# A hybrid encoder block in fp32r: rows of 256 words in the weight ring, a buffer of its own for the first group, and the scores one unit later

## The reference

```python
n1 = rmsnorm(x, norm_mix_g)
q, k, v, o_pre, if_pre, x_r, g_r = split(n1 @ w_in)   # 4 x 1024, 8 gate columns, 2 x 1024
h_m = sigmoid(o_pre) * rmsnorm_per_head(mlstm(q, k, v, i_pre, f_pre))  # 4 heads of 256
h_r = rglru(x_r) * gelu(g_r)                          # 8 blocks of 128
x = x + concat(h_m, h_r) @ w_out                      # 2048 x 2048
gate, up = split(rmsnorm(x, norm_ffn_g) @ w_up)       # 2048 x 2*5632
x = x + (silu(causal_conv3(gate)) * up) @ w_down      # 5632 x 2048
y = rmsnorm(x, norm_final_g)
```

## Time and profile before

| | us |
|---|---|
| median of 3 runs | 1154.48 (1154.33 to 1154.86) |
| the profiled execution | 1154.4 |
| its span, first to last instruction | 1152.6 |
| PE busy | 1140.6 (99%) |
| DVE busy | 746.1 (65%) |
| ACT busy | 578.2 (50%) |
| POOL busy | 51.3 (4%) |
| data moved | 213.56 MB, mean 185 GB/s |

### The profile page before, as it was taken

How to read it: one execution, slowest core, us unless ns; L and a number is a source line. 1 busy time by engine, 2 the same in 40 slices (tenths; PEclk the granted TensorE clock), 3 DMA queues, 4 the chain that set the end, 5 groups by cost and what they waited for, 6 DMA issues and landing times.

```text
span 1152.6 us, 18163 instructions
## 1 busy us (share of the span) xinstructions
PE 1140.6 (99%) x6048; PEld 972.5 (84%) x6048; DVE 746.1 (65%) x985; ACT 578.2 (50%) x769; POOL 51.3 (4%) x47
## 2 busy tenths in 40 slices
PE   8999999999999999999999999999999999999997
PEld 8888888888878888888888888888888888887885
DVE  6668585685866676666666666666666655556554
ACT  7556365463746554444344434444443544455454
POOL 0100100001000000000000000000000000001000
PEclk9999999999999999999999999999999999999999
DMA  8756648566565566566656655655665555555553
GB/s 266 230 147 205 173 142 227 146 195 184 177 204 170 175 195 188 164 195 194 190 156 211 185 180 169 212 183 165 198 195 187 187 189 189 185 187 188 188 184 109
DMA packets 166729, 213.56 MB, mean 185 GB/s; under 512 B 6940, under 2 KB 149660, under 8 KB 166576
## 3 DMA queue, kind: packets, MB, share of 16 engines
q1 hardware_dynamic: 165456, 210.40, 59.0%
q0 software_dynamic: 528, 2.17, 0.5%
q10 hardware_dynamic: 720, 0.67, 0.2%
HBM read 211.10 MB, written 2.11 MB: 185 GB/s over the span
## 4 chain that ended last, share of the span: by engine, by line
PE 91%; DVE 4%; DMA 2%; ACT 2%; issue 1%; SPq 0%; DVEq 0%; ACTq 0%
PE ps L1073 39%; PE ps L1201 27%; PE ps L1075 20%; PE ps L1070 2%; DMA raw<-w_in_dram 2%; DVE w L618 1%; PE ps L1071 1%; ACT w L352 1%; ACT xn L352 1%; PE ps L1171 0%; DVE aT L624 0%; PE ps L1145 0%; PE ps L1045 0%; PE ps L1153 0%; SPq L276 0%
## 5 line engine op out<-in xcount | busy, mean ns | idle before, releaser
L1073 PE MATMUL ps<-xT,w 128*128 128x512 f32 x2048 | 726.7, 398 | 0.0
L618 DVE TENSOR_TENSOR w<-raw,w 128x1024 fp32r<-128x1024 f32 x391 | 479.0, 1238 | 364.7 <-ACT w L352 362.9
L352 ACT ACTIVATE w<-raw 128x1024 fp32r<-128x1024 f32 (+1 forms) x393 | 409.3, 1054 | 434.6 <-PE ps L1075 265.5
L1075 PE MATMUL ps<-xT,w 128*128 128x256 f32 x2048 | 575.9, 281 | 0.0
L1073 PEld LDWEIGHTS ps<-xT,w 128*128 128x128 f32 x2048 | 385.0, 188 | 94.1
L1075 PEld LDWEIGHTS ps<-xT,w 128*128 128x128 f32 x2048 | 386.0, 189 | 0.2
L1201 PE MATMUL ps<-w,aT 128*128 128x512 f32 x1440 | 336.9, 395 | 0.3 <-DVE aT L624 0.2
L1201 PEld LDWEIGHTS ps<-w,aT 128*128 128x128 f32 x1440 | 270.2, 188 | 65.6 <-DVE aT L624 1.2
L352 ACT ACTIVATE fs<-fc 128x512 f32<-128x512 f32 x22 | 13.9, 632 | 101.2 <-DVE fc L967 101.2
L1029 POOL TENSOR_TENSOR fs<-fs,rB 128x512 f32<-128x512 f32 x22 | 28.7, 1305 | 580.4 <-ACT fs L352 580.4
L624 DVE TENSOR_TENSOR aT<-act,aT 128x256 fp32r<-128x256 f32 x88 | 39.0, 443 | 0.0
(11 more groups left out here) (146 smaller groups left out, 402.6 us busy)
## 6 DMA issues: line engine op xcount, KB each, us to landing
raw<-w_up_dram SPq DMA_DIRECT2D x176, 512.0 KB, 4.5
raw<-w_in_dram SPq DMA_DIRECT2D x95, 512.0 KB, 3.9
raw<-w_down_dram SPq DMA_DIRECT2D x88, 512.0 KB, 4.5
raw<-w_out_dram SPq DMA_DIRECT2D x32, 512.0 KB, 4.5
xres<-x_dram SPq DMA_DIRECT2D x3, 512.0 KB, 8.4
y_dram<-xn SPq DMA_DIRECT2D x3, 384.0 KB, 3.1
bc<-rows POOLq DMA_DIRECT2D x4, 256.0 KB, 6.6
gfin<-gfin_dram POOLq DMA_DIRECT2D x1, 1024.0 KB, 5.9
```

The lines of the kernel that those rows point to most:

```text
L352: return sc.activation(out_, in_, fn, **kw)
L618: v.tensor_tensor(w[:, s, :, 1, 0:COLS], raw[:, s, :].rearrange("p (c n) -> p c n", c=CH), w[:, s, :, 0, 0:COLS], ALU.subtract).then_inc(l ...
L1073: mm(full, w[:, s, c, 0, cut], xT[:, kt, :, :].rearrange("p a n -> p (a n)"), start=kt == 0, stop=False)
L1075: ins = mm(rest, w[:, s, c, 1, cut], xT[:, kt, 0, :], start=False, stop=kt == KT - 1)
```

## The change

The ring's rows become 256 words long. The first group gets a buffer of its own, w0, with rows of 272 words for all 16 k-tiles; it lies where tensors of the mixer begin (mixT, gr and others), whose order is changed so that those are in front that are first written later. With that the rounding of group 1 no longer waits for units of group 0 (empty=True).

The first group is fed by single k-tiles: TensorE, ScalarE and VectorE count steps k0 to k15 instead of t0 to t7; the first two k-tiles' weights are rounded and subtracted singly, all others in halves of a unit; and SP loads all units of group 0 in halves. The transposes of bank 1 stand ahead of the first product, the others between tiles or half units. SP issues the first half of the first weights ahead of x 256 to 511. ScalarE issues the identity first; VectorE both rounds and subtracts the gate columns and waits for their transfer; and the rest of the parameters goes to POOL's queue, behind a wait for the last piece of x. VectorE's small instructions on the parameters stand behind the whole of group 0. WARM_UP becomes 6 and KEEP_WARM 2. The scores stand behind unit s == 2 of O.

The diff, cut to its core:

```diff
-WARM_UP, KEEP_WARM = 8, 6
+WARM_UP, KEEP_WARM = 6, 2
...
-        w = sb("w", [P, RING, CH, 2, WROW], F32R)
+        w = sb("w", [P, RING, CH, 2, COLS], F32R)
...
+        first_group = ExitStack()
+        w0 = sb("w0", [P, KT, 2, WROW], F32R, where=first_group)
+        first_group.close()
...
+        def first_place(k):
+            bank = (4, 5, 6, 2)[k] if k < CH else (7, 3, 4, 5, 6, 7)[k // 2 - 2]
+            return ps[:, bank, 0:S] if k < CH else ps[:, bank, k % 2 * S:(k % 2 + 1) * S]
+        def last_in_bank(k):
+            return k if k < CH else k | 1
...
-            load_x(0)
-            sp.wait_ge(lo_ready, 1)
...
+            load_x(0, COLS, x_first_landed)
+            sp.wait_ge(lo_ready, RING)
+            load_first(0, 0, w_first_landed[0])
+            load_x(COLS, BANK, x_landed[0])
+            load_first(0, CH // 2, raw_landed[0])
             for s in range(1, RING):
-                load_x(s)
-                load(0, s, in_v[s, :, :, COL_V:COL_V + COLS], raw[:, s, :].rearrange("p (c n) -> p c n", c=CH))
+                load_x(s * BANK, (s + 1) * BANK, x_landed[s])
+                load_first(s, 0, w_first_landed[s])
+                load_first(s, CH // 2, raw_landed[s])
...
-            def round_units(group, slots=range(RING)):
+            def round_units(group, slots=range(RING), empty=False):
                 for s in slots:
                     act_e.wait_ge(raw_landed[s], group * 16 + 16)
-                    act_e.wait_ge(unit_used, group * RING + s + 1)
+                    if not empty:
+                        act_e.wait_ge(unit_used, group * RING + s + 1)
...
-            act_e.dma_start(par[:, PAR_GMIX + KT:], par_in[:, PAR_GMIX + KT:]).then_inc(par_landed, 16)
...
+            for c in range(CH // 2):
+                x_hi(c)
+                first_hi(0, c, 1, w_first_landed[0], first_hi_ready)
+            for c in range(CH // 2, CH):
+                x_hi(c)
+            first_hi(0, CH // 2, CH // 2, raw_landed[0], hi_ready)
+            for s in range(1, RING):
+                for c, landed, ready in ((0, w_first_landed[s], first_hi_ready), (CH // 2, raw_landed[s], hi_ready)):
+                    for k in range(s * CH + c, s * CH + c + CH // 2):
+                        x_hi(k)
+                    first_hi(s, c, CH // 2, landed, ready)
+                if s < RING - 1:
+                    squares(A0, s - 1, 0)
             squares(A0, 0, 1)
-            round_units(1, [0])
+            round_units(1, [0], empty=True)
...
+            dve.wait_ge(gate_landed, 16)
+            did(v.tensor_copy(w_gate[:, :, 0:2 * H], gate_flat), V0, "gw_hi")
+            after(dve, V0, "gw_hi")
+            did(v.tensor_tensor(w_gate[:, :, 2 * H:4 * H], gate_flat, w_gate[:, :, 0:2 * H], ALU.subtract), V0, "gw_lo")
             dve.wait_ge(gain_landed, 16)
+            for c in range(CH // 2):
+                x_lo(c)
+                dve.wait_ge(first_hi_ready, c + 1)
+                first_lo(0, c, 1, first_lo_ready)
...
+            pool.wait_ge(x_landed[RING - 1], 16)
+            pool.dma_start(par[:, PAR_GMIX + KT:], par_in[:, PAR_GMIX + KT:]).then_inc(par_landed, 16)
             pool.dma_start(tri, const_in[:, C_TRI:C_TRI + P]).then_inc(tri_landed, 16)
...
             transpose_x(0)
             for n in range(KEEP_WARM):
                 mm(ps[:, B_DEN, 0:P], ones[:], ones[:], start=True, stop=True)
+            transpose_x(1)
             pe.wait_ge(group_free, 1)
+            after(pe, V0, "gw_lo")
             pe.wait_ge(first_lo_ready, 1)
-            part_of_unit(0, 0, range(CH // 2), tiles=V0, gated=True)
-            transpose_x(1)
+            part_of_unit(0, 0, [0], tiles=V0)
+            pe.wait_ge(first_lo_ready, 2)
+            part_of_unit(0, 0, [1], tiles=V0)
+            transpose_x(2)
             pe.wait_ge(lo_ready, RING + 1)
...
+            part_of_unit(0, 0, [2], tiles=V0)
             transpose_x(3)
+            part_of_unit(0, 0, [3], tiles=V0).then_inc(unit_used, 1)
+            transpose_x(4)
+            for s in range(1, RING):
+                pe.wait_ge(first_lo_ready, s + 2)
+                part_of_unit(s, 0, range(CH // 2), tiles=V0)
+                if s < RING - 1:
+                    transpose_x(2 * s + 3)
+                pe.wait_ge(lo_ready, s + (1 + RING))
+                part_of_unit(s, 0, range(CH // 2, CH), tiles=V0).then_inc(unit_used, 1)
+                if s < RING - 2:
+                    transpose_x(2 * s + 4)
...
-                    if s == 1:
+                    if s == 2:
                         after(pe, V0, "gcol1")
```

More of the change, by code:

```diff
@@ L424, in _, with x_hi @@
[L424 to L435, removed]
+            def x_hi(k):
+                after(act_e, E0, f"k{last_in_bank(k)}")
+                did(act_fn(xT[:, k, 0, :], first_place(k), scale=par[:, PAR_GMIX + k:PAR_GMIX + k + 1]), A0, f"k{k}")
@@ L689, in _ @@
[L689 to L695 removed]
+            w_gate = w0[:, :, 0, COLS:WROW]
+            gate_flat = gw[:].rearrange("p k a h -> p k (a h)")
@@ new lines, in _, with x_lo @@
+            dve.wait_ge(gate_landed, 16)
+            did(v.tensor_copy(w_gate[:, :, 0:2 * H], gate_flat), V0, "gw_hi")
+            after(dve, V0, "gw_hi")
+            did(v.tensor_tensor(w_gate[:, :, 2 * H:4 * H], gate_flat, w_gate[:, :, 0:2 * H], ALU.subtract), V0, "gw_lo")
+            dve.wait_ge(gain_landed, 16)
+            def x_lo(k):
+                after(dve, A0, f"k{last_in_bank(k)}")
+                did(v.scalar_tensor_tensor(out=xT[:, k, 1, :], in0=first_place(k), scalar=par[:, PAR_GMIX + k:PAR_GMIX + k + 1],
+                                           in1=xT[:, k, 0, :], op0=ALU.mult, op1=ALU.subtract), V0, f"k{k}")
@@ new lines, in first_lo @@
+            def first_lo(s, c, n, ready):
+                tiles = slice(s * CH + c, s * CH + c + n)
+                v.tensor_tensor(w0[:, tiles, 1, 0:COLS], raw[:, s, c * COLS:(c + n) * COLS].rearrange("p (c n) -> p c n", c=n),
+                                w0[:, tiles, 0, 0:COLS], ALU.subtract).then_inc(ready, 1)
+            for c in range(CH // 2):
+                x_lo(c)
+                dve.wait_ge(first_hi_ready, c + 1)
+                first_lo(0, c, 1, first_lo_ready)
+            for c in range(CH // 2, CH):
+                x_lo(c)
@@ new lines, in _ @@
+            dve.wait_ge(hi_ready, 1)
+            first_lo(0, CH // 2, CH // 2, lo_ready)
+            for s in range(1, RING):
+                for k in range(s * CH, s * CH + CH // 2):
+                    x_lo(k)
+                dve.wait_ge(first_hi_ready, s + CH // 2)
+                first_lo(s, 0, CH // 2, first_lo_ready)
+                for k in range(s * CH + CH // 2, (s + 1) * CH):
+                    x_lo(k)
+                dve.wait_ge(hi_ready, s + 1)
+                first_lo(s, CH // 2, CH // 2, lo_ready)
@@ L1054, in spread_rows, with part_of_unit @@
                 did(ins, E, "rB")
-            def part_of_unit(s, pair, tiles_of_k, rows_out=False, tiles=None, gated=False):
+            def part_of_unit(s, pair, tiles_of_k, rows_out=False, tiles=None):
                 for c in tiles_of_k:
                     kt = s * CH + c
-                    if tiles and c % 2 == 0:
+                    if tiles is V0:
+                        after(pe, tiles, f"k{kt}")
+                    elif tiles and c % 2 == 0:
                         after(pe, tiles, f"t{kt // 2}")
@@ L1064, in part_of_unit @@
                         cut = slice(n * P, (n + 1) * P)
-                        if gated:
+                        if tiles is V0:
                             for part, high, end in ((0, 0, WROW), (1, 0, COLS), (0, 1, COLS + 2 * H)):
-                                ins = mm(ps[:, 2 * pair + n, 0:end], xT[:, kt, high, cut], w[:, s, c, part, 0:end],
+                                ins = mm(ps[:, 2 * pair + n, 0:end], xT[:, kt, high, cut], w0[:, kt, part, 0:end],
                                          start=kt == 0 and part == 0 and high == 0, stop=kt == KT - 1 and high == 1)
                         elif rows_out:
-                            mm(full, xT[:, kt, 0, cut], w[:, s, c, :, 0:COLS], start=kt == 0, stop=False)
-                            ins = mm(rest, xT[:, kt, 1, cut], w[:, s, c, 0, 0:COLS], start=False, stop=kt == KT - 1)
+                            mm(full, xT[:, kt, 0, cut], w[:, s, c, :, :].rearrange("p a n -> p (a n)"), start=kt == 0, stop=False)
+                            ins = mm(rest, xT[:, kt, 1, cut], w[:, s, c, 0, :], start=False, stop=kt == KT - 1)
                         else:
@@ L1076, in part_of_unit, with unit @@
                 return ins
-            def unit(g, s, pair, rows_out=False, tiles=None, gated=False):
+            def unit(g, s, pair, rows_out=False, tiles=None):
                 pe.wait_ge(lo_ready, g * RING + (s + 1 + RING))
-                part_of_unit(s, pair, range(CH), rows_out, tiles, gated).then_inc(unit_used, 1)
```

(1 more changed line is left out.)

106 lines of the change are left out of this document (41 added, 65 removed).

## The result

The changed kernel takes 1134.01 us (median of 5 runs, 1133.61 to 1134.90) against 1154.57 in the same comparison: a ratio of 0.9823 (95% interval 0.9809 to 0.9837), 1.8% less. Forecast were 1151.2 us and a range from 1138.5. A few executions came out far slower (one of e14 took 1390 us, at a granted clock of 0.75); they are left out of the comparisons.

The account below looks back on a forecast made before the run. The matmul engine, busy 1140.6 of 1152.6 us, was taken as the bound. From 1154.4, minus 0.9 (start), 1.1 (scores) and 1.2 (rows), came 1151.2 us; the range went from 1138.5 to 1157.

Parts of the forecast that it names:

- The rows of the ring: Matmul pitch with 256-word rows: 0 for the 2048 pairs, 1.2 us gained on L1201 (later L1258), ends 0 and 2.4.
- weight loads from aligned rows: Rival, chance 0.30: pairs loading from the ring fall from 353 to 347.5 ns, 11.3 us gained, 1141.1 us in all.
- even tiles' phase: Rival, chance 0.13: all rows take the even tiles' longer pitch, pairs at 355.5 ns, 5.1 us lost, 1157.5 us.
- Two read ports: Matmul pitch: by the skill's separate ports for streaming and weight loads it would not move, and the sum would be 1152.4.
- The start: Before group 1: first product at 7.3 instead of 8.70, group 1 at 23.2, 0.9 us earlier; bounds 1.6 gained, 1.5 lost.
- The parameters: Start, POOL's queue: land about 20.5, cover 0.6 us before group 1's split; beyond it each us late costs a us.
- the dropped waits: Group 1's rounding no longer waits for used units of group 0; claimed to be worth nothing.
- The clock in the start: Shorter warm-up, 12 records for 16: the clock may rise later, 1.5 us if two tiles run low; taken as nothing.
- transposes at 0.21 us: Sign in the start that would show the prediction wrong; the first transposes were expected at 0.11 us.
- The scores: Head 0, scores moved behind O's third unit: kT is 0.9 us ahead, so the whole 1.1 us wait goes.
- no wait appeared at pv: In head 1, 2 us are left between pT and its product; a new wait at pv would show the prediction wrong.
- The start and scores together: The two gains before group 1 and at head 0's scores: 0.9 us and 1.1 us.

Follow-up runs that it names:

- e14: The e13 kernel with the scores behind O's second unit again; 1139.03 us, ratio interval up to 0.9892.
- e5: Changed kernel with 16 unused words ahead of all tensors, so all begin 64 bytes later at unchanged distances; 1134.88 us.
- e4: Changed kernel with the whole ring, and aT with it, 64 bytes later while xT stays; 1145.55 us.
- e8: Changed kernel with the ring, and aT with it, 256 bytes later while xT stays; 1133.42 us.
- e6: Changed kernel with 16 unused words between the ring and aT, so aT alone begins 64 bytes later; 1142.15 us.
- e10: Changed kernel with the ring 32 bytes further from xT and aT 192 bytes further from the ring; 1148.65 us.
- e11: Changed kernel with the ring 16 bytes further from xT and aT 48 bytes further from the ring; 1142.72 us.
- e1: Changed kernel with only the ring's rows put back to 272 words apart; 1154.17 us, 0.9995 of the kernel before.
- e3: Changed kernel with the scores behind O's second unit again; 1136.32 us, ratio 0.9838.
- e2: Kernel before with the rows alone changed: ring rows of 256 words, first group's weights in w0; 1134.66 us, ratio 0.9826.
- e16: Changed kernel with aT alone 256 bytes later; 1133.44 us.
- e12: Changed kernel with the ring's high and low rows in two planes, the low rows 64 bytes off; 1139.02 us.
- e13: Changed kernel with the ring and aT 16 bytes later, the ring 16 bytes off against xT; 1138.56 us, ratio 0.9868.
- e18: Changed kernel with xT alone moved, so that the ring lies 16 bytes off against it; 1146.01 us, ratio 0.9926.

## Why the prediction was wrong

**The rows of the ring: the step that failed.** "I take 0 for them" for the pairs measured 6.7 ns x 1408 in the up projection, 9.4 us, and the 1.2 us of L1258 measured 9.1. The rival "weight loads from aligned rows" had the pairs nearly right (347.5 ns for 346.3), but priced L1258 with 2.4 us at most, and so its end, 1138.5, became the end of the range. Two readings led there. The first set two kinds of tile against each other within one unit (rows 9 and 10) and took their difference, 5 ns, for the whole that alignment can move. But with rows of 272 words only the high rows of even tiles, one product in four, lay at distance 0 against xT, and those stood in the longer tiles. The difference of two disturbed tiles bounds nothing. The second priced L1258 from the V groups by counting how much of the stream lay in odd tiles. L1258 was a case of its own: no row of the kernel before shows it at another place, so the V groups said little about it, and its ends (0 and 2.4 us, no loss among them) should have been at least as wide as those of the pairs, about 5 ns for each of 1440 instructions, or 7 us either way.

**The cause that this rival named** was half right. Not that loads begin on a multiple (e5), but how the row read as weights lies against the row that is streamed (e4 to e8) makes the difference; why it does is open. The rival on the other side, "even tiles' phase", is refuted by the same windows: pairs at 346.3 where it wanted 355.5.

**Two read ports.** The Trainium skill ("TensorE: Matmul & The Clock Gate", Step-by-step: what each phase is for) says that loading the next weights doesn't take read bandwidth from the running matmul, for there are two ports. By that the pitch would not move, as the prediction set beside its own sum. e6 shows that it does: moving aT, the tensor that L1258 loads, alone by 64 bytes lengthens the matmul by 7 ns, and moving all tensors together (e5) does nothing. The ports may be two; the pitch still depends on both addresses. The Trainium skill's lines of 16 bytes ("SBUF — State Buffer", Door 1: The DMA port swizzle) don't decide it either: 16, 32 and 48 bytes are all whole lines, and 32 (e10, pairs) and 48 (e11, L1258) cost 7 and 8 ns.

**The start.** The first product, put at 7.3, came at 7.56. The engine was through at 22.7 instead of 22.4, then waited 0.81 us for the chain of ScalarE and VectorE as forecast, and group 1, put at 23.2, came at 23.52. The term of 0.9 was 0.55 there, and the new wait ahead of group 2 (0.60 us at 36.17; 0.49 in e1) takes it back, which the sum had not. Nor is the 0.55 steady: in the 18 profiled executions with the changed start group 1 came between 23.25 and 25.36, in nine of them later than the 24.07 of the kernel before, mostly behind waits for x of up to 2.27 us. ScalarE's last rounding came at 21.06 to 22.11, as worked out (21.9). The parameters were there in time, and no trace shows a gain from the dropped waits.

**The clock in the start.** "I take nothing" for the shorter warm-up was wrong in its reason, though it cost little in the changed kernel, where the first product waited 0.35 us for VectorE in any case: one of the prediction's own signs of being wrong, transposes at 0.21 us, came in bank 0. How long the low level lasts differs from one execution to the next: in e8 it was over before the second transpose record, in e5 it held through the first twelve products, which took 2.69 us instead of 1.70 (timeline of PE in e5):

```profile
8.02 2.69 PE L1112 MATMUL ps<-w,xT 128*128 128x272 f32 x12 [0.22 <-DVE w L722]
```

**The scores.** The wait of 1.1 us is gone, the scores began at 56.39 without one, and no wait appeared at pv. That is shown in the trace. But its length at the old place is no constant of the kernel: 1.13 us before, 0.71 in e3, 0.32 in e14 and 0.12 in e2, which had the old order throughout. In the time, e3 and e14 leave the move between nothing and about a microsecond.

**The start and scores together**, 2.0 by the sum, measured 1.7 in e1's profiled execution and 0.6 in its medians, within their interval of nothing.

## What to carry to other kernels

When the matmul engine is busy all the time, read its pitch, not its waits: counts of one line in a long window show a change of 2% that no busy share shows. A pitch that differs between lines of the same shape can be a question of where operands lie. What worked here is to keep the rows read as weights and the rows streamed apart by a multiple of 256 bytes, with every tensor's start a multiple of 64 bytes from the others', and to put odd columns such as gates into a buffer of their own. Any edit that changes the size of a tensor moves all tensors behind it, so compare addresses before giving a gain to the edit.

## What the runs showed of the hardware

The pitch of fp32r matmuls depends on where the two operands lie, by up to 8 ns in 226 (e11) and 7 in 346 (e4), at a granted clock of 1.00. For tensors moved by multiples of 64 bytes it is lowest where both lie at the same place against 256 bytes, and repeats after 256 (e8, e16); pairs of which only the second row is 64 bytes off are as short (e12). At distance 0 the pairs have more than one steady pitch, 347 and 353 ns, and they change from one to the other where other products come between; once in it, they stay until the next such place (changed kernel, e3). e5, e8 and e16, with all distances as in the changed kernel, have their first stretch at 353 ns from about 59 us, behind the scores, and not from 39. With the ring moved by 16 bytes (e11, e13) only the lower one occurred. Why is open; so is what below 64 bytes decides, where e13 and e18 disagree. A run with both operands at the good distance and the mixer always in its lower pitch would stand some 2 us below the changed kernel; none of the runs reached it.
